# The first attention's entry and exit: the last query head's sums and turn ahead of the first scores, and a gate panel in pieces among the last steps

## The reference, cut to what matters

```python
q, k, v, u, ga, gc = jnp.split(h @ lw['w_in'], IN_SPLITS, axis=-1)
q = rmsnorm(q.reshape(B, T, N_Q_HEADS, HEAD_DIM), lw['q_norm_g'])
...
q = apply_rope(q, rope)
k = jnp.concatenate([apply_rope(k, rope), k_ctx], axis=1)
v = jnp.concatenate([v, v_ctx], axis=1)
y_att = attend(q, k, v) @ lw['w_attn_o']
y_conv = conformer_conv(u, lw)
merged = jax.nn.sigmoid(ga) * y_att + jax.nn.sigmoid(gc) * y_conv
return merged @ lw['w_out']
```

## Time and profile before

| what | value |
|---|---|
| median of 3 runs | 2553.55 us (2551.89 to 2563.19) |
| the profiled execution | 2559.04 us |
| its span, first to last instruction | 2557.2 us |
| mean granted TensorE clock | 0.985 |
| busy: TensorE, VectorE, ScalarE, GpSimd | 96%, 66%, 36%, 29% |
| TensorE's scores 0 | 237.73 us from the span's start |
| step 0, value products | 252.70 us |
| gate panel 0, first matmul | 358.23 us |
| gate panel 1, first matmul | 363.77 us |

### The profile page before, as it was taken

How to read it: one execution, slowest core, us unless ns; L and a number is a source line. 1 busy time by engine, 2 the same in 40 slices (tenths; PEclk the granted TensorE clock), 3 DMA queues, 4 the chain that set the end, 5 groups by cost and what they waited for, 6 DMA issues and landing times.

```text
span 2557.2 us, 34962 instructions
## 1 busy us (share of the span) xinstructions
PE 2447.6 (96%) x12016; PEld 2074.2 (81%) x12016; DVE 1682.5 (66%) x3129; ACT 920.1 (36%) x1314; POOL 742.6 (29%) x646
## 2 busy tenths in 40 slices
PE   6999999998999999999998999999999988999998
PEld 4877878686887887888777899999999766788886
DVE  4887769778566766677641368888888785444434
ACT  4223853523233333233322333333333564222222
POOL 0000000000015566676676157777741000000000
PEclk8999999998999999999999999999999999999999
DMA  6222913354234444444445579999998311222321
GB/s 254 92 74 92 353 34 131 116 187 160 89 112 133 139 141 141 141 145 143 132 157 171 190 260 353 362 361 357 363 363 292 104 39 60 92 95 98 99 94 62
DMA packets 177221, 433.59 MB, mean 170 GB/s; under 512 B 32752, under 2 KB 81904, under 8 KB 176752
## 3 DMA queue, kind: packets, MB, share of 16 engines
q1 hardware_dynamic: 123888, 331.61, 37.9%
q0 software_dynamic: 34816, 67.41, 7.6%
q10 hardware_dynamic: 18432, 33.56, 3.4%
HBM read 371.48 MB, written 61.01 MB: 169 GB/s over the span
## 4 chain that ended last, share of the span: by engine, by line
PE 84%; DVE 8%; another core or an unknown queue 3%; ACT 2%; issue 2%; DMA 0%; ACTq 0%; SPq 0%; DVEq 0%
PE ps L478 16%; PE ps L480 16%; PE ps L479 16%; PE ps L811 8%; PE ps L812 8%; PE ps L813 8%; PE ps L724 2%; DVE wlo L1507 2%; DVE ar L1560 1%; PE ps L708 1%; ACT whi L996 1%; PE ps L716 1%; PE ps L548 1%; PE ps L791 1%
## 5 line engine op out<-in xcount | busy, mean ns | idle before, releaser
L1507 DVE TENSOR_TENSOR wlo<-raw,whi 128x1024 fp32r<-128x1024 f32 x426 | 521.4, 1224 | 614.5 <-ACT whi L996 535.2
L2409 POOL DMA_INDIRECT w_scratch<-ar x384 | 419.0, 1091 | 978.0 <-DVE wlo L1507 868.1
L996 ACT ACTIVATE whi<-raw 128x1024 fp32r<-128x1024 f32 x424 | 448.8, 1059 | 659.3 <-PE ps L813 350.1
L478 PE MATMUL ps<-b_hi,whi 128*128 128x512 f32 x1312 | 516.3, 393 | 23.9 <-DVE wlo L1507 23.8
L480 PE MATMUL ps<-b_hi,wlo 128*128 128x512 f32 x1312 | 512.8, 391 | 0.0
L479 PE MATMUL ps<-b_lo,whi 128*128 128x512 f32 x1312 | 512.5, 391 | 0.0
L811 PE MATMUL ps<-a_hi,whi 128*128 128x384 f32 x1024 | 343.2, 335 | 4.6 <-issue 1.6
L813 PE MATMUL ps<-a_hi,wlo 128*128 128x384 f32 x1024 | 342.1, 334 | 0.0
L812 PE MATMUL ps<-a_lo,whi 128*128 128x384 f32 x1024 | 342.1, 334 | 0.0
L478 PE MATMUL ps<-a_hi,whi 128*128 128x512 f32 x816 | 326.4, 400 | 7.7 <-DVE wlo L1507 3.3
L480 PE MATMUL ps<-a_hi,wlo 128*128 128x512 f32 x816 | 319.1, 391 | 0.0
(11 more groups left out here) (269 smaller groups left out, 2933.5 us busy)
## 6 DMA issues: line engine op xcount, KB each, us to landing
raw<-panels SPq DMA_DIRECT2D x430, 512.0 KB
w_scratch<-rstd SPq DMA_DIRECT2D x32, 768.0 KB, 10.8
ar<-w_scratch SPq DMA_DIRECT2D x128, 192.0 KB
ar<-gelu_scratch SPq DMA_DIRECT2D x128, 192.0 KB
ar<-mod SPq DMA_DIRECT2D x32, 512.0 KB, 5.5
gelu_scratch<-ar ACTq DMA_DIRECT2D x64, 256.0 KB
gelu_scratch<-sq ACTq DMA_DIRECT2D x32, 256.0 KB
gelu_scratch<-nt ACTq DMA_DIRECT2D x32, 256.0 KB
```

The lines of the kernel that those rows point to most:

```text
L478: pe.matmul(bank, w_h, hi[:, k, :], start=(k == 0), stop=False)
L996: act.activation(whi[:, u % SPLIT, :], raw[:, u % RAW, :], ACT.Copy).then_inc(hi_ready, 1)
L1507: dve.tensor_tensor(wlo[:, u % SPLIT, :], raw[:, u % RAW, :], f32(whi[:, u % SPLIT, :]), ALU.subtract).then_inc(lo_ready, 1)
L2409: nc.gpsimd.indirect_dma_start(experts, bass.IndirectOffsetOnAxis(offs[:, k:k + 1], 0), vals[:, k:k + 1], None)\
```

## The change

In TensorE's order, `q_stats` and `q_rot` of the last head stand ahead of scores 0. On VectorE the last head's `head_turn` is cut in two: the cosine product stays, sine product and sum come behind the making of `q_scale`; the first reciprocal stands ahead of the memset of `rstd`. ScalarE does an exponential of a single element behind the root of the sums, so that the table load it needs stands there.

Gate panel 0 is cut into four pieces of two blocks (6 matmuls). The first three stand in steps 29, 30 and 31, at the place of the scores that these steps don't have; the fourth follows step 31, ahead of the wait for the whole output. To have the halves of gate panel 1 in time, ScalarE makes its high half behind the last normalisation and VectorE its low half ahead of the last head's split. The first round of the loop over gate panels is written out on TensorE and ScalarE.

```diff
@@ -709,6 +709,16 @@
                 pe.matmul(ps[:, b + 1, 0:CTX], qT[:, h, t * P:(t + 1) * P], kT[:, hu, T:S1], start=True,
                           stop=True).then_inc(sc_ready, 1)
 
+            def first_gate(first, count):
+
+                if first == 0:
+                    pe.wait_ge(lo_ready, AO + (1 - U))
+                    pe.wait_ge(p_ready, ATT - 1)
+                for k in range(first, first + count):
+                    last = split3(ps[:, 0, :], 0, k, a_hi[:, k, :], a_lo[:, k, :], k == 0, k == KT - 1)
+                if first + count == KT:
+                    last.then_inc(used, 1)
+
             def att_step(n):
                 i, hu, t = n // (2 * TT), n // TT % 2, n % TT
                 pe.wait_ge(pn_ready, n + 1)
@@ -717,6 +727,8 @@
                 last.then_inc(pt_ready, 1)
                 if n + 3 < ATT:
                     att_scores(n + 3)
+                else:
+                    first_gate(2 * (n + 3 - ATT), 2)
                 pe.wait_ge(pt_done, n + 1)
                 if t == 0:
                     pe.wait_ge(o_ready, i * 2 + (hu + 1))
@@ -725,20 +737,26 @@
                                      start=(j == 0), stop=(j == ST - 1))
                 last.then_inc(pv_ready, 1)
 
-            att_scores(0)
             q_stats(NH - 1)
             q_rot(NH - 1)
+            att_scores(0)
             att_scores(1)
             att_scores(2)
             for n in range(ATT):
                 att_step(n)
 
 
+            first_gate(KT - 2, 2)
             pe.wait_ge(o_ready, NH + 2)
-            with pe.Fori(0, 2 * KT // 4) as i:
+            def gated_pair(i, u):
+                hi, lo = (a_hi, a_lo) if u % 2 == 0 else (b_hi, b_lo)
+                panel(i * 4 + (AO + u), u, ps[:, u, :], hi, lo, i * 4 + (r_of(AO) + u + 1))
+
+            for u in range(1, 4):
+                gated_pair(0, u)
+            with pe.Fori(1, 2 * KT // 4) as i:
                 for u in range(4):
-                    hi, lo = (a_hi, a_lo) if u % 2 == 0 else (b_hi, b_lo)
-                    panel(i * 4 + (AO + u), u, ps[:, u, :], hi, lo, i * 4 + (r_of(AO) + u + 1))
+                    gated_pair(i, u)
 
 
             def gate_panel(k):
@@ -1077,7 +1095,7 @@
             act.activation(rstd_c, ps[:, 4, 0:CTX], ACT.Sqrt, bias=EPS, scale=1.0 / D).then_inc(rt_ready, 1)
             def gates(first, count, bank_of):
 
-                with act.Fori(0, count // 4) as i:
+                with act.Fori(1, count // 4) as i:
                     for u in range(4):
                         step(i, first, u)
                         if u % 2:
@@ -1135,6 +1153,7 @@
                     head_rt(3, CTX)
             act.wait_ge(kstat, 4 + NH)
             act.activation(q_scale, ps[:, 4, 0:NH * TT], ACT.Sqrt, bias=EPS, scale=1.0 / P).then_inc(krt, 1)
+            act.activation(tiny[:, 54:55], col("zero"), ACT.Exp)
 
 
 
@@ -1170,6 +1189,8 @@
                                ps[:, 4:6, 0:3 * P].rearrange("p a (s n) -> p a s n", n=P), ACT.Copy).then_inc(pt_done, 1)
                 if n + 1 < ATT:
                     att_norm(n + 1)
+                if n == ATT - 2:
+                    hi_next(0, AO, 0)
                 if t == 0 and hu:
                     att_out(i * 2, i, 0)
                 elif t == 0 and i:
@@ -1182,6 +1203,12 @@
                 att_step(n)
             att_out(NH - 1, NH - 1, 1)
 
+            for u in range(4):
+                if u:
+                    hi_next(0, AO, u)
+                act.wait_ge(used, AO + u + 1)
+                if u % 2:
+                    act.activation(sq[:, u // 2, :], ps[:, u - 1, :], ACT.Sigmoid).then_inc(gate_ready, 1)
             gates(AO, 2 * KT, lambda u: u - 1)
 
 
@@ -1675,7 +1702,13 @@
                 dve.wait_ge(kn, n + 1)
 
             def head_turn(m, slot, dst):
+                head_cos(slot)
+                head_sin(m, dst)
+
+            def head_cos(slot):
                 dve.tensor_tensor(q_rot[:, 0, :], q_n[:, slot, :], cos, ALU.mult).then_inc(kcos, 1)
+
+            def head_sin(m, dst):
                 dve.wait_ge(krot, m + 1)
                 dve.tensor_tensor(q_rot[:, 1, :], ps[:, 5, :], sin, ALU.mult).then_inc(ksin, 1)
                 dve.wait_ge(kcos, m + 1)
@@ -1725,7 +1758,10 @@
                 if h < 6:
                     lo(Q + h + 3, h + 3)
                 dve.wait_ge(qn_ready, h + 1)
-                head_turn(h + 2, h % 2, qT[:, h, :])
+                if h < NH - 1:
+                    head_turn(h + 2, h % 2, qT[:, h, :])
+                else:
+                    head_cos(h % 2)
                 if h < 6:
                     early_taps(4)
                 if 1 <= h < 3:
@@ -1777,13 +1813,15 @@
                 elif t == 1 and i:
                     att_lo(i * 2 - 1, i + (NH // 2 - 1), 1)
 
-            for n in range(3):
-                att_max(n)
-                if n == 1:
-                    dve.memset(rstd[:, :], 0.0).then_inc(zeros_ready, 1)
-                    att_recip(0)
+            head_sin(NH + 1, qT[:, NH - 1, :])
+            att_max(0)
+            att_max(1)
+            att_recip(0)
+            dve.memset(rstd[:, :], 0.0).then_inc(zeros_ready, 1)
+            att_max(2)
             for n in range(ATT):
                 att_step(n)
+            lo(AO + 1, 1)
             att_lo(NH - 1, NH - 1, 1)
 
             def last_taps(h):
@@ -1794,7 +1832,6 @@
                     if n == 0:
                         early_taps(1)
 
-            lo(AO + 1, 1)
             for p in range(KT):
                 lo(AO + 2 * p + 2, 2 * p + 2)
                 if p:
```

## The result

| | before | after |
|---|---|---|
| median, 13 executions each | 2560.09 us (2551.67 to 2571.11) | 2545.55 us (2540.90 to 2554.97) |
| ratio after to before | | 0.9943 (95% interval 0.9926 to 0.9960) |
| span of the profiled execution | 2557.2 us | 2541.7 us |
| mean granted clock | 0.985 | 0.986 |

The changed kernel is faster by 0.57%, 14.6 us by the ratio, with an interval from 10.2 to 18.9 us. The forecast was 8.4 us. The time, 2545.55, is 0.4 us from the forecast of 2545.15, but that is luck: the median of before moved up by 6.54 us, from 2553.55 to 2560.09, with more executions, and the medians are 14.54 us apart, 6.14 more than forecast, so two misses cancel. The gain is the thing to judge.

The account below looks back on a forecast made before the run. TensorE bounds the kernel (84% of the chain that ended last), so only its waits matter. Entry 3.6 plus exit 4.8 gives 8.4 us, from 2553.55 to 2545.15 us; range 2540.0 to 2552.0.

Parts of the forecast that it names:

- The entry: Start of attention: third maximum and step 0's value products 3.61 us earlier; 3.6 taken, range 0.6 to 3.6 us.
- the four operations behind the cosine product: VectorE at the entry: the same four operations in another order, 2.00 us from 240.23 to the first maximum at 242.23.
- scores to maximum: Entry, third maximum: starts 1.49 us behind scores 2 if the clock stays up, instead of 2.97 us.
- The wait of TensorE: Entry, before scores 2: TensorE's wait falls from 4.40 to about 2.3 us.
- The clock: Behind the wait before scores 2: forecast stays up; rival says it falls, costing 1.5 us, 6.9 us gained, chance 0.33.
- The exit: End of attention: gate panel 1 starts 4.8 us earlier, at 358.95 instead of 363.77; range 4.0 to 5.5 us.
- value products 1.34 instead of 1.60: Last three steps: value products behind a piece of gate panel 0 take 0.26 us less, as their weights load ahead.
- the slower rhythm: Rival, attention steps: VectorE doing both taps before its maximum lengthens steps 0.7 us each, 2567 us in all; chance 0.04.
- The exit's gain: Rival, end of the gates: VectorE's convolution taps lag, so the 4.8 us are lost and 3.6 left; chance 0.07.
- The table switch: Entry, ScalarE: load off the path saves 1.30 us; rival says the switch costs more, 2544.9 or 2543.75 us, chance 0.02.
- the distance from gate panel 1 to the end unchanged: Sign of a right forecast: everything behind gate panel 1's start takes as long as before.
- fewer falls of the clock elsewhere: Rival, outside the two places: three fewer falls, 1.5 us each, make 12.9 us gained, 2540.65 us; chance 0.05.

Follow-up runs that it names:

- order_only: Kernel before with the entry's new order on TensorE and VectorE, without the advance exponential; one execution, 15.58 us from head 6's turn to step 0's value products (before 16.63).
- entry_only: Kernel before with only the entry's edits, nothing of the gates; ratio to before 0.9997 (0.9982 to 1.0012).
- exit_only: Changed kernel with the entry of before put back, so only the exit's edits; ratio to before 0.9951 (0.9933 to 0.9968).
- third_bank_pair: Changed kernel with scores 2 in PSUM banks 6 and 7, so they don't wait for the first exponential; ratio to before 0.9965 (0.9945 to 0.9985).
- panel_behind: Changed kernel with all 24 matmuls of gate panel 0 behind step 31, none in the steps; ratio to before 0.9951 (0.9926 to 0.9976).
- pieces_123: Changed kernel with gate panel 0 in pieces of 1, 2, 3 and 2 blocks; one execution, 106.35 us from step 0's value products to gate panel 1 (change 105.81).
- same_before: The kernel before, unchanged, measured against itself; ratio 0.9994 (0.9973 to 1.0015).
- change_third: The changed kernel measured a third time, against the kernel before; ratio 0.9945 (0.9926 to 0.9965), span 2558.9 us.
- round_written_out: Kernel before with only the first round of the gate loop written out on TensorE and ScalarE; ratio to before 0.9988 (0.9967 to 1.0009).

## Why the prediction was right, point by point

**The entry** was to gain 3.61 us and gained 3.59 to 3.60 in three profiles of the change and two of the entry alone. By its steps, in the profile's times counted from the turn of head 6 (236.07 before): first maximum predicted at 6.16, measured 6.03; first exponential 7.38 and 7.28; scores 2 8.51 and 8.41; third maximum 10.00 and 10.01; value products 13.02 and 13.03. Two terms were off and cancel: the four operations behind the cosine product took 2.60 us (236.16 to 238.76), not 2.73, and scores to maximum took 1.60 us, not 1.49. So that the value products hit to 0.01 us is luck; the steps themselves are right to some 0.1 us. The wait of TensorE was 1.99 us, predicted 2.3.

**The clock** was the largest uncertainty of the entry and went as forecast, up, in every profile with a wait of 1.99 us. The rival isn't refuted as a mechanism: order_only shows it, with a fall behind 3.26 us.

**The exit** was to gain 4.8 us and gained 5.3. The three distances between value products are 3.44, 3.41 and 3.37 us, before 3.22, 3.17 and 3.16, so 0.22, 0.24 and 0.21 longer. The sum counted each step to the end of its value products, 0.24 longer each; from start to start of the value products that makes 0.50, 0.24 and 0.24, since the first saving of 0.26 comes only with the second value products. What was mis-sized are the two ends, 0.4 us together: the first distance (0.22 instead of 0.50; its wait had been 1.02 us, not the 0.89 that I took from the next ones), and the way from the last value products to gate panel 1, 1.34 + 1.70 = 3.04 by the sum, 2.91 measured (348.66 to 351.57). The term "value products 1.34 instead of 1.60" was read from the chain, whose row starts where the work before it ends (342.26); the timeline has the same value products at 342.10 with 1.50 us. They take 1.50 behind a piece as well, so the term has nearly the right size for the wrong reason. From step 30's value products to step 31's there were 1.44 + 0.82 + 0.90 = 3.16 us (start of the value products to start of the transposes, the transposes, the wait), and there are 1.33 (345.29 to 346.62), 0.58 (to the first matmul of the piece, 347.20, which doesn't wait for the last transpose to end) and 1.46 for the piece, 3.37. So 0.11 came from the value products and 0.24 from the end of the transposes. ScalarE's high half for gate panel 1 delayed nothing: the copy at 347.48 comes 0.86 us behind the transposes' start, as in the step before.

**The sum** of the places was 8.4, measured 8.86. Of the rivals, the slower rhythm did not come: V0 to the last value products is 102.90 us in the change against 102.23 before, and the difference is the 0.7 us of the pieces. The exit's gain was not taken back at the gates: from gate panel 1 to the first matmul behind the wait in the convolution's norm it is 131.80 us before (363.77 to 495.57) and 131.94 in the change (351.57 to 483.51, shown below). The table switch cost its row and no more; the steps were bound as forecast. The forecast gave a gain of more than 0.5% a chance of 0.05, and 0.57% was measured. Its sign "the distance from gate panel 1 to the end unchanged" was a poor one: it is 2193.4 us before and 2190.1, 2189.1 and 2207.3 us in the three profiles of the change.

**What the sum had not got** lies behind the two places. The first part of it is seen, and the forecast had it among its rivals (fewer falls of the clock elsewhere). TensorE waits 2.60 us in the convolution's norm, and before the clock fell behind that wait. In the changed kernel the wait is there,

```profile
483.51 0.47 PE L478 MATMUL ps<-a_hi,whi 128*128 128x512 f32 x1 [2.61 <-ACT ar L1219]
```

and the window around it has a clock of 1.00 (third row of the windows above). From the first gate panel of the convolution to the first expert panel all three profiles of the change take 273.9 to 274.1 us, and before takes 276.4: 2.4 us more. This norm is 1.3 of them (from the low half at 441.84 to that at 504.05 it is 62.2 us, in the change 60.9). The other 1.1 come later, from 548 to 640 us, where TensorE waits 3.55 and 5.00 us for the norm behind the block's output (3.60 and 5.71 in the change). There the clock comes back later in before (windows of before from 620, and of the change from 606, 14 us earlier like the rest):

```profile
620.00:630.00 10.00, 10.00 (x34) 7.65 (x34) 9.52 (x17) 3.38 (x5) 0.00 (x0) 0.74 0.26 90
```

```profile
606.00:616.00 10.00, 9.51 (x41) 7.06 (x40) 9.51 (x17) 4.56 (x6) 0.00 (x0) 1.00 0.25 87
```

This isn't bound to either half alone (entry_only 276.5, exit_only 276.6), nor does it come with every kernel that has both: third_bank_pair has it (274.2), panel_behind doesn't (276.4), and pieces_123 has only the later part (275.5). What decides it stays open. 8.9 + 2.4 = 11.3 us lie inside the measured interval of 10.2 to 18.9.

The second part stays open. All three ratios of the change are near 0.9945, 14 us, and both exit_only and panel_behind measured 0.9951, 12.5 us, where their places give 5.9 and 5.5 us, some 0.9978; the entry alone measured 0.9997 and 0.9996, 3 us less than its place but within its intervals. Kernels measured together share their executions of before, but the surplus isn't an accident of those: exit_only's median is also 11.9 us below that of same_before, measured beside it. The profiles don't show these 3 to 7 us: the expert layer, in which a single execution wanders by 20 us, has the same average with and without the exit.

The record has one more trace of it, the mean granted clock of every timed execution. In the three later sets, within one kernel, an execution with a clock higher by 0.001 was 2.6 us shorter (157 executions, correlation -0.77). The executions of exit_only and panel_behind had a clock 0.0015 and 0.0021 above those of before, by that slope an estimated 4 and 5 us of the 7 us that each has too much. But change_third measured its 14 us with a clock only 0.0008 above. So the clock is at most a part, and nothing shows why it should be higher with the exit, or whether it is cause or consequence. Written-out code alone (0.9988) doesn't account for it. And third_bank_pair, which has all of the exit and the 2.4 us behind it, measured 0.9965, a smaller gain than the 12.0 us (0.9953) that these give, though 0.9953 is inside its interval; so the surplus may as well be chance in the sets of executions. The intervals, some 5 us to either side, leave both open.

## What to carry to other kernels

Price a reordering from the timeline of the place, step by step from one fixed event, and compare profiles by the same distance; whole spans of this kernel wander by twice the gain. Where a wait of TensorE of 3 to 4 us is shortened, count also what runs behind it: here 1.4 of 3.6 us were the clock that no longer fell. Independent matmuls in a wait cost less than their own length beyond it: 1.46 us of them in a wait of 0.90 made the step 0.21 us longer, not 0.56, since the ends of the matmuls around them overlap too. A piece that is shorter than the wait is hidden whole: 3 matmuls in a wait of 1.02 us left the step at 3.23 us, where it was 3.22.

## What the runs showed of the hardware that was not expected

Waits of TensorE of nearly the same length went either way: the clock was down behind 4.40 us in three profiles with this wait (before, same_before, round_written_out) and partly in the fourth (exit_only), down behind 3.26 us, up behind 3.12 and 1.99 us at the same place of the program, and up behind 2.52 us a few matmuls later (third_bank_pair); and behind 2.60 us in the convolution's norm it was down in the kernel before and up in the changed one (up in all three profiles of the change and in third_bank_pair, down in the other ten). The Trainium skill, "TensorE: Matmul & The Clock Gate", part 1, has the half clock as the state of rest, at 1.2 GHz; the traces agree, with scores taking 2.07 us instead of 1.02 for the pair behind a fall.

One and the same kernel left profiles whose spans differ by 17 us, twice the 8.9 us that were gained at the two places, while those places themselves repeat to 0.05 us. It lies in the expert layer, where TensorE waited 22.5 us in the shortest of these profiles and 37.1 us in the longest.
